# Router products in two column halves, attention values in twelve loads, and two early score steps in one encoder layer

## The reference, cut to what matters

```
# neighbourhood attention: rows of 64 grid columns, 8 heads of 64; four blocks of 16 query columns,
# each sees 32 key columns that start at column 0, 8, 24, 32, in up to 8 grid rows around its own
s = einsum('bnqhd,brnchd->bhnqrc', q_row, k_rows[kcol]) * scale
p = softmax(where(mask, s + bias, -inf))
o = einsum('bhnqrc,brnchd->bnqhd', p, v_rows[kcol])
...
# router: 4 group logits and 32 expert logits for each token, then top-1 group and top-2 experts
g_prob   = softmax(xf @ w_rg)        # w_rg: 1024 x 4
e_logits = xf @ w_re                 # w_re: 1024 x 32
```

## Time and profile before

| What | us |
|---|---|
| median of 3 runs | 1205.43 |
| lowest and highest | 1205.01, 1205.53 |
| the profiled execution, its own time | 1207.23 |
| its span in the profile | 1205.6 |
| PE busy in it | 1145.1 (95%) |
| DVE busy | 644.6 (53%) |
| ACT busy | 469.7 (39%) |

### The profile page before, as it was taken

The page is one execution under the profiler, slowest core; times in us unless marked ns, Lnnn a source line. Parts: engine busy times, 40 slices in busy tenths (PEclk is TensorE's granted clock), DMA queues, the critical chain, the costliest instruction groups (busy, mean ns, idle before and its releaser), DMA issues.

```text
span 1205.6 us, 19051 instructions
## 1 busy us (share of the span) xinstructions
PE 1145.1 (95%) x6884; PEld 918.3 (76%) x6884; DVE 644.6 (53%) x1245; ACT 469.7 (39%) x983; POOL 232.6 (19%) x337
## 2 busy tenths in 40 slices
PE   8999999999998999999999999999986999999956
PEld 6888888878885666888898887778776788887722
DVE  6332333312116896333566663754667998884256
ACT  6333333211015785111333333544224666764223
POOL 2322322200000000000100000100022334554344
PEclk9999999999999999999999999999986999999979
DMA  9573553843148425523222002822896999989967
GB/s 323 131 261 111 146 164 99 291 99 95 48 113 219 110 53 169 184 76 94 63 76 71 1 24 78 300 82 94 330 334 237 370 372 352 358 299 358 405 256 273
DMA packets 108429, 226.61 MB, mean 188 GB/s; under 512 B 28854, under 2 KB 48318, under 8 KB 108222
## 3 DMA queue, kind: packets, MB, share of 16 engines
q1 hardware_dynamic: 83822, 167.86, 41.3%
q0 software_dynamic: 17856, 43.02, 10.7%
q10 hardware_dynamic: 6672, 14.69, 3.9%
HBM read 180.89 MB, written 69.78 MB: 208 GB/s over the span
## 4 chain that ended last, share of the span: by engine, by line
PE 82%; DVE 4%; DMA 4%; issue 3%; SPq 2%; ACT 2%; POOL 1%; DVEq 0%; POOLq 0%; ACTq 0%
PE bank L576 18%; PE bank L578 17%; PE bank L577 17%; PE bank L2361 5%; PE bank L2289 3%; PE bank L2158 3%; PE bank L2327 3%; PE bank L2144 2%; PE bank L2131 2%; PE bank L2347 2%; PE bank L2298 2%; PE bank L2223 2%; PE bank L2399 2%; DMA at<-in_w_in 2%; DVE at L571 1%
## 5 line engine op out<-in xcount | busy, mean ns | idle before, releaser
L576 PE MATMUL bank<-at,at 128*128 128x512 f32 (+1 forms) x1192 | 441.9, 371 | 4.3 <-DVE at L571 2.7
L578 PE MATMUL bank<-at,at 128*128 128x512 f32 (+1 forms) x1192 | 432.0, 362 | 0.0
L577 PE MATMUL bank<-at,at 128*128 128x512 f32 (+1 forms) x1192 | 431.3, 362 | 0.0
L576 PEld LDWEIGHTS bank<-at,at 128*128 128x128 f32 x1192 | 226.1, 190 | 39.0 <-DVE at L571 3.7
L578 PEld LDWEIGHTS bank<-at,at 128*128 128x128 f32 x1192 | 225.9, 189 | 34.9
L577 PEld LDWEIGHTS bank<-at,at 128*128 128x128 f32 x1192 | 226.1, 190 | 32.3
L571 DVE TENSOR_TENSOR at<-at,at 128x1024 fp32r<-128x1024 f32 (+2 forms) x162 | 180.5, 1127 | 104.6 <-ACT at L566 101.8
L566 ACT ACTIVATE at<-at 128x1024 fp32r<-128x1024 f32 (+2 forms) x162 | 154.2, 985 | 165.5 <-DVE at L1545 49.0
L899 POOL TENSOR_TENSOR at<-at 128x1 f32<-128x1 f32 x88 | 24.2, 275 | 553.8 <-ACT at L1264 278.1
L2361 PE MATMUL bank<-at,at 128*128 128x512 f32 x156 | 74.2, 597 | 3.3 <-ACT at L1338 3.3
L995 POOL DMA_INDIRECT y_tok<-at,at x39 | 39.4, 1010 | 132.3 <-DVE at L1902 92.7
(11 more groups left out here) (224 smaller groups left out, 1326.3 us busy)
## 6 DMA issues: line engine op xcount, KB each, us to landing
at<-in_w_exp_gate SPq DMA_DIRECT2D x39, 512.0 KB, 7.6
at<-in_w_exp_up SPq DMA_DIRECT2D x39, 512.0 KB, 11.1
at<-in_w_exp_down SPq DMA_DIRECT2D x39, 512.0 KB, 13.1
at<-y_tok SPq DMA_DIRECT2D x24, 512.0 KB, 10.6
at<-in_w_in SPq DMA_DIRECT2D x6, 1024.0 KB, 11.4
xT_hi_all<-at POOLq DMA_DIRECT2D x12, 512.0 KB, 3.9
xT_lo_all<-at POOLq DMA_DIRECT2D x12, 512.0 KB, 5.7
at<-xT_hi_all SPq DMA_DIRECT2D x3, 2048.0 KB, 10.1
```

The source lines that it names most:

```text
L576: nc.tensor.matmul(out, w_hi, x_hi, start=(k == 0), stop=False)
L577: nc.tensor.matmul(out, w_lo, x_hi, start=False, stop=False)
L578: last = nc.tensor.matmul(out, w_hi, x_lo, start=False, stop=(k == len(terms) - 1))
```

## The change

Three places. First, the router: each of the 8 products of a router group becomes two, with 64 tokens each as weights, which write to partitions 0 to 63 and 64 to 127 of the same accumulator, one half of the array's columns each. Second, the values: `v_att` is stored as (256 tokens of a group, 6 groups, 512), so that the rows of two adjacent groups lie next to each other (4 KB); `vals` is reordered so that the two groups of a part lie next to each other for each column block; and each part is 4 transfers onto all 128 partitions, whose source is 4 grid rows x 32 columns x 4 KB. Third, score step 1 is computed together with step 0 ahead of the last query/key chunk, which goes to bank 7 instead of 3, and its exponentials follow at once on ACT. Beside this the bias copies are cut differently between the channel loads: 9, 8, 12, 12, 7, 0 calls instead of 14, 10, 10, 10, 4, 0.

```diff
-        v_att = dram("v_att", [T, HALF])
+        v_att = dram("v_att", [GTOK, NKG, HALF])
...
-        def val_rows(part, n, r):
-            groups = slice(2 * part, 2 * part + 2)
-            src = v_att[2 * part * GTOK:2 * (part + 1) * GTOK].rearrange("(g r c) d -> r c g d", r=QROWS, c=GW)
-            dst = vals.rearrange("p (g n) d -> p n g d", n=4)[r * KC:(r + 1) * KC, n, groups]
-            return dst, src[r, COL_START[n]:COL_START[n] + KC]
+        def val_rows(part, n):
+            src = v_att.rearrange("(r c) g d -> r c g d", r=QROWS)[:, COL_START[n]:COL_START[n] + KC, 2 * part:2 * part + 2]
+            dst = vals[:, 8 * part + 2 * n:8 * part + 2 * n + 2]
+            return dst, src
+
+        def val_tile(kg, n):
+            return 8 * (kg // 2) + 2 * n + kg % 2
...
-            for tile, first, past in zip(channels, (0, 14, 24, 34, 44, 48), (14, 24, 34, 44, 48, 48)):
+            for tile, first, past in zip(channels, (0, 9, 17, 29, 41, 48), (9, 17, 29, 41, 48, 48)):
...
             for n in range(4):
-                for r in range(QROWS):
-                    sp.dma_start(*val_rows(0, n, r)).then_inc(vals_here[0], 16)
+                sp.dma_start(*val_rows(0, n)).then_inc(vals_here[0], 16)
             sp.wait_ge(chunk1_done, 2)
             for n in range(4):
-                for r in range(QROWS):
-                    sp.dma_start(*val_rows(2, n, r)).then_inc(vals_here[2], 16)
+                sp.dma_start(*val_rows(2, n)).then_inc(vals_here[2], 16)
...
-                act.dma_start(v_att[bass.ds(t * P, P)], v_st[j]).then_inc(v_stored[j], 16)
+                act.dma_start(v_att[j * P:(j + 1) * P, bass.ds(i, 1)], v_st[j].unsqueeze(1)).then_inc(v_stored[j], 16)
...
                         for n in range(4):
-                            for r in range(QROWS):
-                                act.dma_start(*val_rows(1, n, r)).then_inc(vals_here[1], 16)
+                            act.dma_start(*val_rows(1, n)).then_inc(vals_here[1], 16)
...
-            for s in range(N_STEPS + 1):
+            exps(0)
+            exps(1)
+            evac_pT(0)
+            for s in range(2, N_STEPS + 1):
...
-                        nc.vector.tensor_copy(*channel_chunk(2 * i + j, 0, bank[3 * j][:])).then_inc(qk_evac_v[j], 1)
+                        nc.vector.tensor_copy(*channel_chunk(2 * i + j, 0, bank[7 * j][:])).then_inc(qk_evac_v[j], 1)
                         if j == 0:
                             scores(0)
+                            scores(1)
...
-                mm = split_products(bank[3 * j + n][:], [...
+                mm = split_products(bank[7 if then_values and j == 1 and last else 3 * j + n][:], [...
...
                         scores(0)
+                        scores(1)
...
-                    pe.wait_ge(vals_here[part], 16 * 4 * QROWS)
+                    pe.wait_ge(vals_here[part], 16 * 4)
...
-                                                    vals[:, 4 * kg + 2 * (s % 2) + n, hp * P + half * HD:hp * P + (half + 1) * HD],
+                                                    vals[:, val_tile(kg, 2 * (s % 2) + n), hp * P + half * HD:hp * P + (half + 1) * HD],
...
-            for s in range(1, N_STEPS + 2):
+            for s in range(2, N_STEPS + 2):
...
-                        b = b[:, 0:NG + NE]
-                        steps = [(r_T[t % 2][:, k], w_rt[:, k]) for k in range(KT)]
+                        for k in range(KT):
+                            for tok in (slice(0, P // 2), slice(P // 2, P)):
+                                mm = nc.tensor.matmul(b[tok, 0:NG + NE], r_T[t % 2][:, k, tok], w_rt[:, k], start=(k == 0), stop=(k == KT - 1))
+                        mm.then_inc(mm_done, 1)
+                        continue
```

More of the change, by code:

```diff
@@ L1195, in split_y_tile @@
                 make_hi(act, split_y(t), y_hi[j], y_T[j])
-            for s in range(N_STEPS + 1):
+            exps(0)
+            exps(1)
+            evac_pT(0)
+            for s in range(2, N_STEPS + 1):
                 if s < N_STEPS:
                     exps(s)
-                if s >= 1:
-                    evac_pT(s - 1)
+                evac_pT(s - 1)
                 if s in W_OUT_STEPS:
@@ L1555, in split_y_tile @@
                 make_lo(dve, split_y(2 * i + j), y_lo[j], y_T[j], y_hi[j])
-            for s in range(N_STEPS + 2):
-                if 0 < s < N_STEPS:
+            evac_pT(0)
+            for s in range(2, N_STEPS + 2):
+                if s < N_STEPS:
                     scores(s)
@@ L1561, in _ @@
                     evac_yT(0, 0)
-                if 1 <= s <= N_STEPS:
+                if s <= N_STEPS:
                     evac_pT(s - 1)
@@ L1566, in _ @@
                     make_lo(dve, split_w_out(n, k), w_out_lo[n][:, k], w_out[n][:, k], w_out_hi[n][:, k])
-                if s >= 2:
-                    evac_o(s - 2)
+                evac_o(s - 2)
                 if s in (N_STEPS - 2, N_STEPS - 1):
@@ L2075, in channel_chunk @@
             def channel_chunk(j, n, last, then_values=False):
-                mm = split_products(bank[3 * j + n][:], [(w_qk_hi[j][:, k], w_qk_lo[j][:, k], xT_hi[n][:, k], xT_lo[n][:, k])
+                mm = split_products(bank[7 if then_values and j == 1 and last else 3 * j + n][:], [(w_qk_hi[j][:, k], w_qk_lo[j][:, k], xT_hi[n][:, k], xT_lo[n][:, k])
                                                          for k in range(KT)])
@@ L2180, in _ @@
                     transpose_y(0, 0)
-                if 2 <= s <= N_STEPS:
+                if s <= N_STEPS:
                     transpose_p(s - 1)
-                if s >= 2:
-                    values(s - 2)
+                values(s - 2)
             def out_tile(i, j, last):
@@ L2285, in _ @@
                         pe.wait_ge(nt_evac, 2 * (n_norms["moe", t] + 1))
-                        b = b[:, 0:NG + NE]
-                        steps = [(r_T[t % 2][:, k], w_rt[:, k]) for k in range(KT)]
+                        for k in range(KT):
[3 more added lines that the diff above has]
+                        continue
                     for k, (w, x) in enumerate(steps):
-                        mm = nc.tensor.matmul(b if kind == "route" else b[:], w, x, start=(k == 0), stop=(k == len(steps) - 1))
+                        mm = nc.tensor.matmul(b[:], w, x, start=(k == 0), stop=(k == len(steps) - 1))
                     mm.then_inc(mm_done, 1)
```

## The result

| | before | after |
|---|---|---|
| median, us | 1205.01 | 1236.02 |
| lowest and highest | 1203.95, 1205.53 | 1235.63, 1240.55 |
| the profiled execution's own time | 1207.23 | 1235.63 |
| its span | 1205.6 | 1234.0 |
| mean granted clock of PE | 0.978 | 0.967 |

The ratio is 1.0257, 95% interval 1.0242 to 1.0272: 31 us slower, where 25.6 were forecast. (Both kernels ran here side by side, so the median of before is a little off the 1205.43 of the first table.)

What follows compares the result with a forecast made beforehand. PE, busy 95% of the span, was taken as the bound, with values only just hidden. Late values 28.0 + 1.0 - 3.4 for the router = +25.6 us, so 1205.4 becomes 1231 us, range 1207 to 1240.

Steps and rivals of the forecast that it cites:

- four shared engines at 25.6 GB/s: Value loads: all twelve share four DMA engines, 102 GB/s together, so 6.29 MB take 61.4 us; chance 0.74.
- The rival of 16 engines: Value loads use all 16 engines, nothing waits, early scores and router gain in full: 1197 us; chance 0.17.
- about 8 engines: Value loads: from about 8 engines on, transfers end at 379.4, just ahead of evac_o(4) at 380.11; at 6 the change loses.
- each queue has four engines of its own: Value loads, rival: SP's eight transfers take 41.0 us and end at 389.7, +5.2 us, 1210.6 us; chance 0.06.
- the term of 28.0 us: Attention: late values and the store behind them put evac_o(4) at 411.0 and scores(7) at 411.3, 28.0 us later.
- scores(7), now at 383.35: DVE's order in attention: the step behind evac_o(4), taken to move from 383.35 to 411.3, giving the delay of 28.0 us.
- The 1.0 us in the sum: Attention: 1.0 us added to the forecast sum beside the 28.0 us delay.
- Early scores and channel load: Query/key chunks and first attention steps: channel load -1.5 us, 5.3 us in all with early scores; swallowed if values are late.
- The wait at 265: First channel load, issued up to 6.4 us earlier: PE's 1.5 us wait for the DVE weight split near 265 disappears.
- 5.3 us "if the values have landed": First attention steps: channel load 1.5, values(0) earlier by 1.9 + 0.8, two following steps 1.1; needs landed values.
- Router: 3.4 us forecast: Router stage: 0.46 us less per group on six tiles, plus half for the last two: -3.4 us (from -6 to +3).
- The rival in which half-width products get slower: Router: 65 ns a pair at full clock adds 3.0 us: 1237 us with four engines, 1203 with sixteen; chance 0.1.

Runs made afterwards that it cites:

- e13_windows: Changed kernel with four copies first laying the column windows out one after another in memory, then twelve loads from 128 adjacent rows: 1196.96 us, ratio 0.9928.
- e2_cols12: Changed kernel, twelve value loads kept, column instead of grid row outermost in the source (values meet other keys' probabilities): 1191.58 us, ratio 0.9873.
- e3_cols8: Changed kernel with 48 loads of eight columns by four grid rows, column outermost (other keys' probabilities): 1199.55 us, ratio 0.9950 of the kernel before.
- e7_rows2: Changed kernel with 24 value loads of two grid rows (64 partitions) instead of twelve of four: 1297.47 us, ratio 1.0751 of the kernel before.
- e6_scores: Kernel before with only the early scores and the other division of the bias copies: 1205.36 us, ratio 0.9993.
- e11_values: Kernel before with only the values' part, twelve loads with the column outermost (other keys' probabilities): 1199.28 us, ratio 0.9940.
- e4_router: Kernel before with only the router's part of the change: 1202.39 us, ratio 0.9964.
- e14_half: The version with windows laid out in memory, its twelve loads cut into 24 of 64 partitions: 1201.84 us, ratio 0.9973 of the kernel before.
- e1_rows48: Changed kernel with the values in 48 loads of one grid row (32 partitions) instead of twelve: 1201.89 us, ratio 0.9959 of the kernel before.
- e12_cols16: Changed kernel with 24 loads of 16 columns by four grid rows, column outermost, 64 partitions (other keys' probabilities): 1197.36 us, ratio 0.9920.
- e10_by_col: Changed kernel with twelve column-outermost loads and exponentials writing probabilities in that key order with a stride: 1205.39 us, ratio 0.9998 of the kernel before.

## Why the prediction was right, and where its sum was off

The direction, the likeliest case and its mechanism were right; the time, 1236.0, is 5 us above the 1231 forecast and inside the range. What was off are sizes, and one row that was read as another.

**Engines of a load: right.** The term of four shared engines at 25.6 GB/s stands: 103 to 106 GB/s in the windows, values(0) at 387.85 where "at about 390" was written. Four was the author's estimate, one engine for each grid row. That `in_g_mix` has no landing time where `in_sgu_b` has one was weak support: loads that nothing changed can lack one, as `in_w_exp_gate` in the changed kernel and `in_sgu_b` itself in e13_windows. The rival of 16 engines is what e2_cols12 and e13_windows show when the outermost count is 32 or 128 (shares of 1.01 and 1.00). Its turning point, "about 8 engines", is what e3_cols8 shows: less the expert block, it ties with the kernel before. That each queue has four engines of its own is excluded by 103 GB/s with both queues at work, and e7_rows2 excludes it for two.

**When the attention goes on: the term of 28.0 us was too small by 5.2.** Two steps of it failed. First, "scores(7), now at 383.35" named the wrong row, as does the heading of the earlier trace rows. Behind evac_o(4) at 380.11, DVE's timeline of the kernel before has the bias step of scores(7):

```profile
380.76 0.56 DVE L1513 CUSTOM_DVE_ANT_0 at<-bank,at 128x384 f32<-128x384 f32 x1 [0.37 <-PE bank L2131]
```

The one at 383.35 is that of scores(8), one step later. That is 2.6 us. Second, the store of group 0 was given 0.9 us behind the last values; it landed at 413.62, and evac_o(4) started at 413.74 instead of 411.0: 2.7 us. Whether the values ended later than reckoned or the store took longer behind them stays open, since the values have no landing time in this trace. With both, 413.95 - 380.76 = 33.2 us. The 1.0 us in the sum was the author's estimate for the steps behind PE's idle time, and no run shows it by itself. What the changed kernel shows in its place is a granted clock of 0.50 from 370 to 390 us and from 413 to 418, 1.12 us for the 16 instructions of values(0) where 16 take 0.62 at 393.29, 1.51 us for 6 transposes at 416.32 where 6 take 0.80 at 420.12, and the end of the attention 34.4 us late, 1.2 more than the 33.2.

**Early scores and channel load: right, swallowed.** The wait at 265 went as described. That the two are worth 5.3 us "if the values have landed" is seen in e13_windows and e2_cols12, whose attention ends 5.4 and 5.6 us earlier. In e6_scores, with the values landing as before, it is 0.8, and in e11_values, with fast values and no early scores, 0.1.

**Router: 3.4 us forecast, 4.3 measured** (3.0 to 5.7, e4_router). A group of 32 instructions takes 1.06 us on the chain where 1.09 were worked out:

```profile
842.32 1.06 PE bank L2290 x32
```

From one group's start to the next it is 10.19 us (842.32 to 852.51) where it was 10.70 (808.04 to 818.74): 0.51 less, against the 0.46 worked out. So the six groups were priced well; the rest of the difference is within the interval, and which of the last six groups give it was not taken apart. The rival in which half-width products get slower falls.

**The sum again:** 33.2 + 1.2 - 4.3 = 30.1 us, against 31.0 measured (29.2 to 32.8 by the interval). What is left is within it.

## What to carry to other kernels

Count the outermost dimension of a load's source before its partitions or its bytes: a load of four rows of a grid ran at a quarter of the rate (103 GB/s), and exchanging two dimensions gave it all back (393). Then keep it on all 128 partitions, since half of them gave 228 GB/s where all gave 389. A load on the way to a first use also stands ahead of the stores issued behind it (the store that evac_o(4) waited for took 17.03 us to land, where the median is 2.1), so its price has to be followed through the next buffer that waits to be free. And two improvements that wait for the same thing can each measure as nearly nothing (0.8 and 1.5 us, both within the noise) and be worth some 5 us together: here early scores and faster values, tested one at a time, would both have been dropped.

An experiment that computes something else can change the amount of work where the work depends on the data; compare the counts of a late stage before its time is believed.

## What the runs showed of the hardware that was not expected

- **Half of the partitions, half of the rate.** With all 16 engines busy, loads onto 32 or 64 partitions moved 224 to 234 GB/s between 350 and 360 us, and onto 128 partitions 389 to 396. e13_windows against e14_half (389 and 228) has the same bytes, the same 4 KB pieces and the same source. A load of the one is 512 KB and of the other 256, but loads of 128 and of 256 KB had the same rate (224 in e1_rows48, 226 in e12_cols16). With 8 engines busy, loads onto 32 partitions still got 25.6 GB/s from each. So it looks like a limit of about 230 GB/s on what such loads take in; the 205 GB/s of eight engines lie just below it, and the kernel before sat at it, too. No run here shows where the limit lies or why it is the same for 32 and 64.
- **Issues are held up behind a narrow load.** In the changed kernel the issuing instructions of the values take far longer than before, when those on ACT took 328 to 485 ns each. The view of v_att (ns min/median/max to issue):

```profile
L1157 ACTq DMA_DIRECT2D at<-v_att x4: 686/944/10545, 346.2 to 348.9; - x4
L707 SPq DMA_DIRECT2D at<-v_att x4: 581/608/6082, 346.3 to 348.2; - x4
L710 SPq DMA_DIRECT2D at<-v_att x4: 6859/8696/9889, 357.1 to 383.6; - x4
```

  SP is held from 357.12 to 391.39 by four instructions. Nothing was due on SP in that time, as evac_o(1), which the first store waits for, ended at 392.45. ACT's four hold it from 346.24 to 359.45, and its next copy, 0.60 us, starts at 359.50, where it starts at 357.08 in e2_cols12. That cost nothing here, because PE had work until 365 and then waited for the values anyway. In e13_windows the same twelve issues take 0.32 to 0.76 us each.
- **ACT's exponentials are slower when they write with a stride of 16 bytes**: 996 ns against 608 for 128x384, 760 against 501 for 128x256 (e10_by_col against e2_cols12). They also write to another buffer there, where e2_cols12 writes in place; that was not tried apart.
